# First weight panels multiplied on the unnormalised residual, with the RMS factor applied when the product leaves PSUM

## The reference, cut to what matters

```
def _rmsnorm(x, g, eps=NORM_EPS):
    xf = x.astype(jnp.float32)
    y = xf * lax.rsqrt(jnp.mean(xf * xf, axis=-1, keepdims=True) + eps)
    return (y * g.astype(jnp.float32)).astype(x.dtype)

    # end of the first block, start of the second
    return _rms_norm(h, norm_final)
    ...
    h = _rmsnorm(x, norm_mix[l])
    p = h @ w_in[l]                       # 1024 x (RWKV + MLA + DIFF + gates)
    ...
    x = x + merged @ w_o[l]
    x = x + _conv_ffn(_rmsnorm(x, norm_ffn[l]), ffn_w_up[l], ...)
```

## Time and profile before

| | |
|---|---|
| median of 3 runs | 2359.54 us (2354.59 to 2359.70) |
| the profiled execution | 2362.72 us, of which the span of the trace is 2361.4 us |
| TensorE matmuls | 2257.7 us busy, 96% of the span |
| VectorE, ScalarE, GpSimd | 64%, 40% and 16% |
| mean granted TensorE clock | 0.984 of full |

### The profile page before, as it was taken

How to read it: one execution, slowest core, us unless ns; L and a number is a source line. 1 busy time by engine, 2 the same in 40 slices (tenths; PEclk the granted TensorE clock), 3 DMA queues, 4 the chain that set the end, 5 groups by cost and what they waited for, 6 DMA issues and landing times. The chain is left out here.

```text
span 2361.4 us, 36947 instructions
## 1 busy us (share of the span) xinstructions
PE 2257.7 (96%) x14328; PEld 1914.6 (81%) x14328; DVE 1501.5 (64%) x2311; ACT 954.9 (40%) x1534; POOL 367.7 (16%) x365
## 2 busy tenths in 40 slices
PE   6999999999999999999999999979999999998998
PEld 4888887666678888878888876669998998898998
DVE  4666766565675666666565346556667766876874
ACT  4222223455442222242222244545446334555763
POOL 1000001000000000000000010039995476000000
PEclk9999999999999999999999999999999999999999
DMA  7554445111134444434443242124544232244544
GB/s 280 190 189 178 171 165 178 72 37 54 54 134 160 168 175 170 169 119 178 160 177 129 98 129 80 55 87 154 191 168 167 94 115 73 90 146 158 179 175 144
DMA packets 52615, 331.03 MB, mean 140 GB/s; under 512 B 6545, under 2 KB 7825, under 8 KB 21649
## 3 DMA queue, kind: packets, MB, share of 16 engines
q1 hardware_dynamic: 49040, 319.15, 37.4%
q0 software_dynamic: 3456, 10.25, 1.5%
HBM read 325.56 MB, written 3.80 MB: 139 GB/s over the span
## 5 line engine op out<-in xcount | busy, mean ns | idle before, releaser
L1183 PE MATMUL bank<-u_hi,whi 128*128 128x512 f32 (+1 forms) x2512 | 867.6, 345 | 32.5 <-DVE u_lo L1137 14.9
L1184 PE MATMUL bank<-u_lo,whi 128*128 128x512 f32 (+1 forms) x2512 | 848.7, 338 | 0.0
L1185 PE MATMUL bank<-u_hi,wlo 128*128 128x512 f32 (+1 forms) x2512 | 848.1, 338 | 0.0
L568 DVE TENSOR_TENSOR wlo<-raw,whi 128x2048 fp32r<-128x2048 f32 (+2 forms) x207 | 433.3, 2093 | 317.0 <-ACT whi L566 317.0
L1183 PEld LDWEIGHTS bank<-u_hi,whi 128*128 128x128 f32 x2512 | 477.2, 190 | 108.9 <-issue 29.5
L1185 PEld LDWEIGHTS bank<-u_hi,wlo 128*128 128x128 f32 x2512 | 477.5, 190 | 51.6
L1184 PEld LDWEIGHTS bank<-u_lo,whi 128*128 128x128 f32 x2512 | 477.8, 190 | 48.8 <-issue 0.2
L566 ACT ACTIVATE whi<-raw 128x2048 fp32r<-128x2048 f32 (+2 forms) x207 | 353.1, 1706 | 340.6 <-PE bank L1185 254.0
L1245 ACT ACTIVATE sil<-bank 128x512 f32<-128x512 f32 (+1 forms) x88 | 47.8, 544 | 541.7 <-PE bank L1185 541.7
L1183 PE MATMUL bank<-hidden_hi,whi 128*128 128x512 f32 x528 | 205.4, 389 | 0.0
L1184 PE MATMUL bank<-hidden_lo,whi 128*128 128x512 f32 x528 | 205.4, 389 | 0.0
(11 more groups left out here) (426 smaller groups left out, 2907.2 us busy)
## 6 DMA issues: line engine op xcount, KB each, us to landing
raw<-in_stream SPq DMA_DIRECT2D x231, 1024.0 KB, 4.8
raw<-in_stream SPq DMA_DIRECT2D x80, 704.0 KB, 4.0
first_ada<-in_stream SPq DMA_DIRECT2D x8, 1024.0 KB, 16.4
raw<-in_stream SPq DMA_DIRECT2D x8, 768.0 KB, 4.3
skew<-rpb_rows POOLq DMA_DIRECT2D x8, 336.0 KB, 6.2
nbr_bias<-skew POOLq DMA_DIRECT2D x24, 112.0 KB, 3.5
h<-in_tokens SPq DMA_DIRECT2D x1, 2048.0 KB, 11.5
uq_ukv<-in_small POOLq DMA_DIRECT2D x1, 1536.0 KB, 8.0
```

The lines of the kernel that those rows point to most:

```text
L568: v.tensor_tensor(self.lo[to][:, 0:n], raw[:, 0:n], self.hi[to][:, 0:n].bitcast(F32), ALU.subtract).then_inc(self.s_lo, 1)
L1183: pe.q.matmul(dst, w[0], x[0], start=start, stop=False)
L1184: pe.q.matmul(dst, w[0], x[1], start=False, stop=False)
L1185: return pe.q.matmul(dst, w[1], x[0], start=False, stop=stop)
```

## The change

At both norms the first panel is multiplied on "raw" operands. While the phase before is evacuated, each new residual chunk is also scaled by the gain and split into `u_raw_hi` (ScalarE) and `u_raw_lo` (VectorE). TensorE multiplies chunks 0 to 2 of the panel before the sums of the norm, chunks 3 to 5 behind them and before the spread of the factor, and 6 and 7 after it. Behind the norm VectorE copies the factor from its bank to SBUF, and the evacuation of a raw panel multiplies by it. At the first norm the second panel (`RAW_PANELS = 2`) is multiplied on raw operands too. The four `wlo` quarters of the second panel stand together behind the diagonals. In `side_panels` the split of panel 2 moves ahead of the evacuation of panel 0, and `dense(2)` / rows / `dense(1)` becomes `dense(5)` / rows with `dense(1)` between.

```
+    def raw_chunk(c, gain, k):
+        act.q.activation(u_raw[0][:, c, :], h[:, c, 0:S], ACT.Copy, scale=gain).then_inc(s_raw_hi, 1)
+        dve.q.wait_ge(s_raw_hi, k.plus(1))
+        dve.q.scalar_tensor_tensor(out=u_raw[1][:, c, :], in0=h[:, c, 0:S], scalar=gain,
+                                   in1=u_raw[0][:, c, :].bitcast(F32), op0=ALU.mult, op1=ALU.subtract).then_inc(s_raw_lo, 1)
+
+    def first_on_raw(then, dst, freed):
...
+        def early():
+            pe.q.wait_ge(st.s_lo, ph.first + 1)
+            pe.q.wait_ge(st.s_ev, freed)
+            for kc in range(3):
+                chunk(kc)
+
+        def late():
+            for i in range(1, 4):
+                st.split_hi(ph, 1, i)
+            for i in range(4):
+                st.split_lo(ph, 1, i)
+            for kc in range(3, 6):
+                chunk(kc)
+
+        def rest():
+            chunk(6)
+            return chunk(7)
...
@@ norm_scale, behind the diagonals
+        if late:
+            late()
@@ down
             if m.static() and m.base == KC - 1:
                 marks = residual_parts(at(m), banks[2 * par], n, lambda s: gates(m, s), G)
-                last_squares(n, marks, k, weighted, then)
+                last_squares(n, marks, k, weighted, None if raw_gains is not None else then)
+                if raw_gains is not None:
+                    raw_chunk(KC - 1, raw_gains[:, KC - 1:KC], Count(r0 + KC - 1))
+                    st.split_hi(PHASE[then], 1, 0)
                 return
...
             add_square(at(m), n, count=k, weighted=weighted)
+            if raw_gains is not None:
+                raw_chunk(at(m), raw_gains[:, bass.ds(m.plus(0), 1)], Count(r0 + m.base, m.step, m.reg))
@@ between the blocks
-    ready = norm(1, lambda c, s: (both_gains[:, c:c + 1], None), "rwkv_in", twice=True)
+    early, late, side_first = first_on_raw("rwkv_in", banks[raw_bank:raw_bank + 2], st.groups - 1)
+    early()
+    rd = norm_scale(S, True, None, late)
+    ready = norm(1, lambda c, s: (both_gains[:, c:c + 1], None), None, twice=True, rd=rd)
+    factor_ready = copy_factor(rd[1], banks[5])
@@ side_evac
-                copied = act.do(act.q.activation(buf[:, 1:S + 1], side_target(n, b), ACT.Copy))
-                r = act.q.activation(mix[:, c, :], side_target(n, b), ACT.Copy, scale=rest_mu[:, c:c + 1])
+                if n < RAW_PANELS:
+                    dve.q.wait_ge(st.s_pe, PHASE[name].first + k + 1)
+                    dve.after(factor_ready)
+                    copied = dve.do(dve.q.tensor_tensor(buf[:, 1:S + 1], side_target(n, b), factor, ALU.mult))
+                    act.after(copied)
+                else:
+                    copied = act.do(act.q.activation(buf[:, 1:S + 1], side_target(n, b), ACT.Copy))
+                r = act.q.activation(mix[:, c, :], buf[:, 1:S + 1] if n < RAW_PANELS else side_target(n, b), ACT.Copy,
+                                     scale=rest_mu[:, c:c + 1])
@@ side_panels
-                if q == 0 and n >= 1:
+                if q == 0 and n >= 1 and n != 1:
                     side_flush(n)
                 name, k = side_list[n + 1] if n + 1 < len(side_list) else ("branch", 0)
                 if n < 16:
                     if q == 0 and n > 0:
                         st.split(PHASE[name], Count(k))
+                    if q == 0 and n == 1:
+                        side_flush(n)
@@ the hand-written order
+    dense(5)
     for i in range(4):
-        dense(2)
         x2 = scaled_rows("norm_final", [], range(2 * i, 2 * i + 2))
-    dense(1)
+        dense(1)
@@ wo_evac
+        for c in (2 * m.base, 2 * m.base + 1):
+            raw_chunk(c, vcol("norm_ffn_2", c), Count(raw_count[0] + c))
@@ up_evac, first panel only
+                act.after(dve.do(dve.q.tensor_tensor(cu[par][:, b, 2:S + 2], banks[2 * par + b][:, 0:S], factor, ALU.mult)))
```

78 lines of the change are left out of this document (60 added, 18 removed).

## The result

| | before | after |
|---|---|---|
| median of the runs | 2358.72 us (2354.59 to 2359.70, 4 runs) | 2379.59 us (2376.18 to 2381.63, 4 runs) |
| ratio after / before | | 1.0088, 95% interval 1.0075 to 1.0101 |
| profiled execution, its span | 2362.72, 2361.4 us | 2381.63, 2380.2 us |

The change makes the kernel 20.9 us slower by the times and 18.8 us by the two spans. The forecast was 2370.5 us in a range of 2361 to 2376: the sign and the mechanism at the first norm came true, the size (+11.0 us forecast) is too small by almost half.

What follows compares the result with a forecast made beforehand. The prediction took TensorE, busy for 96% of the span, as the bound; its terms +0.3 +8.9 +2.2 -0.4 +0 = +11.0 us on a median of 2359.5 gave 2370.5 us, range 2361 to 2376.

Steps and rivals of the forecast that it cites:

- (a): Down projection: eight raw copies and products, mostly covered by VectorE's waits, +0.3 us; some 2 us if stretched beside GpSimd.
- (b) to (d): First norm: later sums, four `wlo` quarters together, then the norm proper from 1798.8, lasting 8.5 us, ending at 1807.3.
- (e) to (g): Behind first norm: split of panel 2, evacuations and `h` rows delay the tanh to 1824.1 against 1815.19, +8.9 us.
- (f): Behind first norm: panel 0 evacuated in halves of 1.45 us, then eight `h` rows, then panel 1, to 1820.1.
- (h): Behind the first norm's tanh: TensorE at half clock after standing 4 to 8 us, +2.2 us (0 to 2.4).
- (i): Behind that product: a slowed TensorE no longer waits 0.41 us for ScalarE at 1829.02, -0.4 us.
- Norm 2: Second norm: panel 2 starts at 2174.9 behind its low part, evacuations not late; 0 us, from -1 to +3.
- Rival 3: Slower yet: raw products stretch beside GpSimd, clock falls in waits at both norms; +15 us, 2374.5 us, chance 0.12.

Runs made afterwards that it cites:

- raw_unused: Kernel before plus the down projection's raw copies and products, read by nobody, and the product of the gains taken early: 2359.18 us, ratio 0.9999.
- rows_behind: Changed kernel with VectorE's eight `h` rows moved behind the evacuation of panel 1: 2374.49 us, ratio 1.0060.
- one_raw_panel: Changed kernel with only panel 0 raw at the first norm; panel 1 uses normed rows and ScalarE alone evacuates it: 2373.28 us, ratio 1.0059.
- split_before_norm: Changed kernel with three raw panels and the split of panel 2 ahead of the norm proper: 2381.58 us, ratio 1.0098.
- filled_waits: Changed kernel with 56 and 58 products nobody reads in TensorE's two waits at the first norm: 2374.51 us, ratio 1.0063.
- norm2_only: The change at the second norm alone, everything up to `w_o` as in the kernel before: 2363.20 us, ratio 1.0015.
- norm2_mended: norm2_only with the table load behind panel 2's high part and VectorE's two factor products ahead of its low part: 2360.22 us, ratio 1.0003.
- changed_again: The changed kernel measured once more, nothing altered: 2377.15 us, ratio 1.0076.
- before_filled: Kernel before with 13 products nobody reads in TensorE's three waits at the first norm: 2359.04 us, ratio 0.9998.
- filled_mended: norm2_mended with 13 products nobody reads in TensorE's waits at the first norm: 2358.81 us, ratio 0.9994.
- gains_early: Changed kernel with `both_gains` computed ahead of the norm of the last feed-forward: 2377.01 us, ratio 1.0086.
- all_mends: Changed kernel with rows_behind, gains_early, filled_waits (56 and 33 products) and the order of norm2_mended together: 2367.39 us, ratio 1.0035.
- norm_later: Five raw panels, first norm proper in five steps in the branch, `h` rows behind them, early gains, order of norm2_mended: 2378.00 us, ratio 1.0075.

## Why the prediction came out 10 us short

- **(a) raw operands, 0.3 us.** Covered, as said; `raw_unused` shows no cost at all. By the page "SBUF — State Buffer" of the Trainium skill (section "Who interferes with whom") the products beside a GpSimd that reads SBUF are held up, and they are (0.76 us against 0.48). None took more than 0.81 us, though, while GpSimd's instructions beside them have means of 1.07 to 1.46 us; that one is blocked until the other ends is not what these rows show, as far as GpSimd's rough spans can tell. The 2 us of the sum that I gave for that rule did not come, since VectorE's waits before the splits take it.
- **Not in the sum: the gate on `both_gains`, 1.0 us.** I priced the work of the down projection and not the two new waits that the diff puts ahead of it.
- **(b) to (d), the norm.** Counted from the end of the projection (1.4 us later than before) the norm started at 1798.2 (1798.8 predicted) and lasted 9.05 us, from `sil` to `one_less_mu` (8.5). The two misses cancel: it ended at 1807.25 (1807.3).
- **(e) to (g), +8.9 us: right.** Panel 2 at 1811.9 on the clock of before (1811.7 predicted), TensorE idle 7.65 us (7), tanh at its end 1824.2 (1824.1); +9.0 in the pair of profiles. `rows_behind`, `one_raw_panel` and `split_before_norm` show the mechanism: taking the rows out of the list moves the product by 2.9 us, taking panel 1's factor and the rows out by 4.0, taking away TensorE's own wait of 7.65 us by 1.1. That the end came out within 0.1 us has luck in it: in (f) the three parts and two hand-overs of 0.10 us add up to 1.63 us and not to the 1.45 that I wrote; the halves came every 1.5 us, as the next one overlaps.
- **(h) the clock, +2.2 us, (i) -0.4: the mis-sized term, and the largest part of the miss.** The two together, 1.8 us in the sum, measured 4.85 us. I took the length of the half clock behind the one poorly filled stretch of before, 4.60 us; here 11 of its 13.6 us (1823.0 to 1836.6) fell behind the tanh, after TensorE had stood for 7.65 and then 6.57 us with only 36 matmuls between. Hardly anything was absorbed: TensorE's wait ahead of the token sums fell from 0.41 to 0.16 us, since ScalarE was late too. `filled_waits` gives all of it back.
- **Norm 2, 0 us: the step whose mechanism failed.** It measured +2.4 us in the first pair of profiles (over all profiles the stretch is 165.0 to 166.1 us with the change and 161.8 to 162.7 without) and +3.5 by the times of `norm2_only`. I let the low part of panel 2 release TensorE at 2174.9. It did so at what would be 2174 on that clock, but the same TensorE instruction list also waits for the evacuation of panel 0, whose bank pair panel 2 reuses. I wrote that evacuations are not late there; the evacuation of panel 0 had gained a hand-over and stood behind the split, and TensorE waited 5.25 us for it where I had 3.7 for the low part. Of the 2.4 us, 0.75 are the later start of panel 2 and 1.6 come with the half clock behind it, which I had priced only in the bound of +3 us. `norm2_mended` shows the cause: the two moves behind the norm alone shorten the wait from 5.26 to 2.22 us.
- The two profiles differ by 18.8 us where the sum has 11.0: 3.0 of the difference are (h) and (i), 2.4 the second norm, 0.9 half clock and waits in the branch, 0.7 stand ahead of the down projection, 0.4 in it and 0.4 at the end. The rest, some 2 us up to the 20.9 of the first comparison, is within what two sets of runs differ by: `changed_again` has a ratio of 1.0076, 17.9 us.

Rival 3 (+15 us) had the clock behind all waits and at norm 2 in it, but no evacuation, and its own condition, the stretched raw products, cost nothing. The range ended at 2376 in part because the clock's term had been bounded at 2.4 us by a single row.

## What to carry to other kernels

A gain on the engine that is bound (here 5 us of TensorE) was worth nothing at a place where two other engines' in-order lists meet it: walk those lists to the next instruction it must wait for, before pricing anything. A product taken out of the wait must be paid where its factor comes back, and there it was put on an engine that had the split and the rows queued ahead. Where a change makes TensorE stand for several microseconds, price the half clock behind it up to the whole next stretch, and list every semaphore that the waiting instruction needs, bank reuse too, not only the operand's.

## What the runs showed of the hardware

- **A short half clock can cost more than half its length.** Between the token sums and the panel that waits for its low part, the profiles with no half clock in that stretch (raw_unused, before_filled, filled_mended, rows_behind, gains_early, filled_waits, split_before_norm) have 20.9 to 21.1 us and those with 3.4 us of it 22.5 to 23.8. Half of 3.4 us is 1.7. The rest is the panel's transfer: in the kernel before it is issued 13.4 us behind the token sums and ScalarE can split it 5.9 us later, in `before_filled` 11.8 and 4.9 us, and TensorE waits 2.67 us for the low part where it hardly waits in the other. Both profiles of the kernel before and both of the changed one have the half clock there, so whether executions of one program fall on either side, and whether this is part of the 8 us by which runs of the kernel before differ (2355.0 to 2363.3), is not shown.
- **The length of a wait did not tell how much half clock stood behind it.** Behind the product that waits for the tanh the half clock ended 11.0 us later in the changed kernel (waits of 7.65 and 6.57 us), 10.8 in `changed_again` (7.43 and 5.14), 8.4 in `gains_early` (8.18 and 6.23), 9.3 in `split_before_norm` (one of 14.74) and 9.6 in `one_raw_panel` (3.01, with 3.10, 1.46 and 1.10 ahead of it). These are single profiles. `filled_waits`, with both waits filled, has none between 1598 and 2018 us.
- **One profile of `all_mends` has another matmul pace.** In `up_2` a panel of 48 matmuls came every 5.44 us, in the sixteen others every 5.65 us, all at full clock; over the last 19 of the 22 panels that is the 3.9 us by which its norm 2 stretch is shorter than those of `filled_mended` and `norm_later`, which have the same order and the same 3.4 us of half clock. No cause was found. Whether its other five runs had this pace is not on record; if all had, `all_mends` without it would be some 12 us slower than before.
